# First and last expert item of a mixture-of-experts block: transposes into the result banks, earlier splits, and the last weights in other slots

## The reference

```python
def moe_ffn(h, w_router, b_router, w_gu, b_gu, w_down, b_down):   # top-4 of 32 experts
    ...
    gates = jax.nn.softmax(top_vals, axis=-1)
    ...
    def expert_block(args):
        xb, e = args
        gu = xb @ w_gu[e] + b_gu[e]                     # 1024 -> 2048
        gate, lin = gu[:, :D_EXPERT], gu[:, D_EXPERT:]
        gate = jnp.minimum(gate, 7.0)
        lin = jnp.clip(lin, -7.0, 7.0)
        act = (lin + 1.0) * (gate * jax.nn.sigmoid(1.702 * gate))
        return act @ w_down[e] + b_down[e]              # 1024 -> 1024
```

## Time and profile before

| what | value |
|---|---|
| median of 3 runs | 1746.84 us (1746.36 to 1748.47) |
| the profiled execution | 1746.15 us |
| its span in the trace | 1744.3 us |
| PE busy | 1647.6 us, 94% of the span |
| DVE, ACT, POOL busy | 62%, 48%, 8% |
| chain that ended last | PE 90%, DVE 4%, ACT 3%, DMA 2% |
| items begin, items' last scatter begins | 531.7 us, 1724.4 us |

### The profile page before, as it was taken

The page is one execution under the profiler, slowest core; times in us unless marked ns, Lnnn a source line. Parts: engine busy times, 40 slices in busy tenths (PEclk is TensorE's granted clock), DMA queues, the critical chain, the costliest instruction groups (busy, mean ns, idle before and its releaser), DMA issues.

```text
span 1744.3 us, 26775 instructions
## 1 busy us (share of the span) xinstructions
PE 1647.6 (94%) x9998; PEld 1373.1 (79%) x9998; DVE 1075.8 (62%) x1139; ACT 831.2 (48%) x844; POOL 134.8 (8%) x220
## 2 busy tenths in 40 slices
PE   6999989999966799999999999999999999999994
PEld 5876657987745688888888888888888888888882
DVE  4221553434255677777777777776777767777773
ACT  4243364434221455555546555455455554555543
POOL 0020220000000000100001000010000100001001
PEclk9999999999977899999999999999999999999997
DMA  5111123422065799999999999999999999999965
GB/s 201 49 49 49 48 97 121 145 82 79 24 261 203 240 361 365 384 364 370 369 371 373 365 375 365 368 386 369 360 371 372 375 374 365 369 370 377 364 247 162
DMA packets 134773, 477.05 MB, mean 273 GB/s; under 512 B 10242, under 2 KB 10291, under 8 KB 134707
## 3 DMA queue, kind: packets, MB, share of 16 engines
q1 hardware_dynamic: 123968, 446.72, 68.6%
q0 software_dynamic: 7168, 25.17, 6.2%
q10 hardware_dynamic: 3602, 4.69, 0.8%
HBM read 457.67 MB, written 18.87 MB: 273 GB/s over the span
## 4 chain that ended last, share of the span: by engine, by line
PE 90%; DVE 4%; ACT 3%; DMA 2%; issue 1%; ACTq 0%; SPq 0%; POOL 0%; DVEq 0%; POOLq 0%
PE psum L977 23%; PE psum L996 21%; PE psum L1019 21%; PE psum L609 17%; PE psum L788 1%; PE psum L777 1%; PE psum L971 1%; PE psum L963 1%; PE psum L765 1%; PE psum L880 1%; PE psum L900 1%; ACT ring_split L1116 1%; PE psum L914 0%; DVE ring_split L1496 0%; DMA X<-in_x 0%
## 5 line engine op out<-in xcount | busy, mean ns | idle before, releaser
L977 PEld LDWEIGHTS psum<-MIX,ring 128*128 128x128 f32 x4096 | 774.9, 190 | 100.9 <-DVE MIX L1904 0.9
L977 PE MATMUL psum<-MIX,ring 128*128 128x96 f32 x4096 | 725.6, 259 | 0.2 <-DVE MIX L1904 0.2
L1871 DVE TENSOR_TENSOR ring_split<-ring,w_hi_a 128x2048 fp32r<-128x2048 f32 x64 | 146.5, 2289 | 88.4 <-ACT w_hi_a L1363 86.6
L1877 DVE TENSOR_TENSOR ring_split<-ring,w_hi_x 128x2048 fp32r<-128x2048 f32 x64 | 146.5, 2288 | 88.3 <-ACT w_hi_x L1372 88.3
L996 PE MATMUL psum<-ring_split,xs_hi 128*96 128x512 f32 x512 | 200.3, 437 | 0.0
L1019 PE MATMUL psum<-ring_split,act_hi 128*96 128x512 f32 x512 | 199.0, 436 | 0.0
L1871 DVE TENSOR_TENSOR ring_split<-ring,w_hi_x 128x2048 fp32r<-128x2048 f32 x64 | 146.4, 2289 | 74.2 <-ACT w_hi_x L1363 74.2
L609 PE MATMUL psum<-ring_split,H_hi 128*128 128x512 f32 (+1 forms) x512 | 151.8, 380 | 0.6 <-DVE ring L1582 0.6
L1877 DVE TENSOR_TENSOR ring_split<-ring,w_hi_a 128x2048 fp32r<-128x2048 f32 x64 | 146.2, 2285 | 3.5 <-ACT w_hi_a L1372 3.5
L1372 ACT ACTIVATE w_hi_a<-ring 128x2048 fp32r<-128x2048 f32 x64 | 121.7, 1901 | 7.0 <-DMA ring<-in_w_down 7.0
L1372 ACT ACTIVATE w_hi_x<-ring 128x2048 fp32r<-128x2048 f32 x64 | 121.8, 1904 | 2.6 <-DMA ring<-in_w_down 2.6
(11 more groups left out here) (284 smaller groups left out, 2647.1 us busy)
## 6 DMA issues: line engine op xcount, KB each, us to landing
ring<-in_w_gu SPq DMA_DIRECT2D x256, 1024.0 KB, 10.2
ring<-in_w_down SPq DMA_DIRECT2D x128, 1024.0 KB, 12.1
ring<-in_w_in SPq DMA_DIRECT2D x6, 2048.0 KB, 10.5
X<-in_x SPq DMA_DIRECT2D x8, 512.0 KB, 7.9
ring<-in_w_out SPq DMA_DIRECT2D x2, 2048.0 KB, 7.7
ring<-in_w_mk SPq DMA_DIRECT2D x2, 2048.0 KB, 9.0
ring<-in_w_mv SPq DMA_DIRECT2D x2, 2048.0 KB, 7.8
ring<-in_w_mq SPq DMA_DIRECT2D x2, 2048.0 KB, 7.7
```

The costliest lines, as they stand in the source:

```text
L977: return mm(psum[:, dst, q * C:(q + 1) * C], lhsT=gate_w(k // 2)[:, k % 2, f * P:(f + 1) * P], rhs=xsT[:, k, :], start=k == 0 and q == 0, ...
L1871: v.tensor_tensor(lin_lo(c), lin_w(c), chunk_hi(c).bitcast(F32), ALU.subtract)\
L1877: v.tensor_tensor(down_lo(c), down_w(c), chunk_hi(c).bitcast(F32), ALU.subtract)\
```

## The change

On PE, `item_transpose(1)` moves to after the third lin chunk of item 0 and writes banks 6 and 7, and its wait for `s_ltt` goes. The wait for `y_out(31)` goes, and the last down writes banks 2 and 3, with its lo parts in the lin slots. SP loads the last down chunks into the lin slots, each once `lin` chunk c of item 31 is multiplied. ACT loads its table and makes `xs_hi` of item 0 before it waits for the accumulator's stores, and its first and last item are reordered; `y_out_last` reads banks 2 and 3 and writes `lin_rows`. DVE splits two lin chunks ahead of `xT_next(0)` and reads its register later; in the first item `xT_next(1)` comes early, and `xT_lo(1)` before `activate(0, 0)`. POOL gathers the first four items straight from `src_row`, without index copies, the first ahead of its register read.

```diff
@@ SP @@
-                sp.wait_ge(s_dused, 4 * m + c + 1)
-                load_down(d, c)
+                sp.wait_ge(s_lused, 4 * m + c + 1)
+                sp.dma_start(lin_w(c), down_rows(d, c)).then_inc(s_m[8 + c], 16)
@@ PE @@
-            def item_transpose(t):
+            def item_transpose(t, to=T0):
...
                     x_last.then_inc(s_lused, 1)
+                    if c == 2 and isinstance(t, int) and t == 0:
+                        item_transpose(1, Y0)
...
-            def down_chunk(v, c, gate):
+            def down_chunk(v, c, gate, lo=down_lo, to=Y0):
...
             lin_transpose(0)
-            pe.wait_ge(s_ltt, 1)
-            item_transpose(1)
             lin_and_gate(1)
...
             down_and_gate(m, transpose_next=False)
-            pe.wait_ge(s_yrow, m)
             for c in range(4):
-                down_chunk(m + 1, c, False)
+                down_chunk(m + 1, c, False, lin_lo, L0)
@@ ACT @@
             def lin_hi(t, c):
                 act.wait_ge(s_m[8 + c], 16 * t + 16)
-                if not isinstance(t, int) or t > 0:
+                if isinstance(t, int):
+                    if t > 0:
+                        act.wait_ge(s_lused, c + 1)
+                else:
                     act.wait_ge(s_dused, 4 * t + c - 3)
...
             def down_hi(v, c, last=False):
-                act.wait_ge(s_m[c], 16 * v)
                 if last:
+                    act.wait_ge(s_m[8 + c], 16 * v + 16)
                     act.wait_ge(s_dused, 4 * v + c - 3)
+                    go(chunk_hi(c), lin_w(c), ACT.Copy).then_inc(s_dhi, 1)
...
+            def y_out_last(v):
+                go(gate_last, slot_gate[:, bass.ds(v - 1, 1)], ACT.Copy).then_inc(s_gcur, 1)
+                act.wait_ge(s_gcur, v)
+                act.wait_ge(s_dused, 4 * v + 4)
+                go(lin_rows.rearrange("p (a b) -> p a b", a=2), psum[0:C, 2:4, :], ACT.Copy,
+                   scale=gate_last).then_inc(s_yrow, 1)
...
+            nc.scalar.preload_act_table_set("sigmoid_and_others")
+            xT_hi(0)
             act.wait_ge(s_accinit, 16 * TT)
+            lin_hi(0, 2)
+            lin_hi(0, 3)
             act.wait_ge(s_items, 1)
             m = act.value_load(last_item_i[0:1, 0:1], min_val=E - 1, max_val=MAX_ITEMS - 1)
-            nc.scalar.preload_act_table_set("sigmoid_and_others")
-            xT_hi(0)
-            lin_hi(0, 2)
-            lin_hi(0, 3)
+            lin_hi(1, 0)
+            lin_hi(1, 1)
             lin_out(0)
+            xT_hi(1)
             sigmoid(0, 0)
-            xT_hi(1)
-            lin_hi(1, 0)
+            lin_hi(1, 2)
             a_hi(0, 0)
-            lin_hi(1, 1)
-            lin_hi(1, 2)
+            lin_hi(1, 3)
             sigmoid(0, 1)
-            lin_hi(1, 3)
...
             down_hi(m + 1, 2, last=True)
+            sigmoid(m, 1)
+            down_hi(m + 1, 3, last=True)
+            a_hi(m, 1)
             y_out(m)
-            sigmoid(m, 1)
-            a_hi(m, 1)
-            down_hi(m + 1, 3, last=True)
-            y_out(m + 1)
+            y_out_last(m + 1)
@@ DVE @@
-            m = dve.value_load(last_item_i[0:1, 0:1], min_val=E - 1, max_val=MAX_ITEMS - 1)
             lin_lo_part(0, 0)
+            lin_lo_part(0, 1)
             xT_next(0)
             xT_lo(0)
             xT_place(0)
-            for c in range(1, 4):
-                lin_lo_part(0, c)
+            m = dve.value_load(last_item_i[0:1, 0:1], min_val=E - 1, max_val=MAX_ITEMS - 1)
+            lin_lo_part(0, 2)
+            lin_lo_part(0, 3)
+            xT_next(1, 6)
+            lin_lo_part(1, 0)
+            lin_lo_part(1, 1)
             st = Steps(0)
             bias(st, 0)
             gate_in(st, 0, 0)
             lin_in(st, 0)
+            xT_lo(1)
             activate(st, 0, 0)
-            xT_next(1)
-            lin_lo_part(1, 0)
-            xT_lo(1)
+            xT_place(1)
             a_lo(0, 0)
-            xT_place(1)
-            lin_lo_part(1, 1)
             lin_lo_part(1, 2)
...
-            down_lo_part(m + 1, 0)
+            last_down_lo_part(m + 1, 0)
             a_lo(m, 0)
-            down_lo_part(m + 1, 1)
-            down_lo_part(m + 1, 2)
+            last_down_lo_part(m + 1, 1)
+            last_down_lo_part(m + 1, 2)
             gate_in(st, m, 1)
             activate(st, m, 1)
             a_lo(m, 1)
-            down_lo_part(m + 1, 3)
+            last_down_lo_part(m + 1, 3)
@@ POOL @@
+            def first_gather(t):
+                if t > 0:
+                    pool.wait_ge(s_xt, t)
+                g.indirect_dma_start(out=x_rows, out_offset=None, in_=rows_dram[:, :],
+                                     in_offset=bass.IndirectOffsetOnAxis(src_row[:, t:t + 1], 0))\
+                    .then_inc(s_xrow, 16)
...
+            pool.wait_ge(s_rowsout, 16 * TT)
+            pool.wait_ge(s_items, 1)
+            first_gather(0)
+            n = pool.value_load(n_items_i[0:1, 0:1], min_val=E, max_val=MAX_ITEMS)
...
-            scatter(late + 3)
+            scatter(late + 3, lin_rows)
             pool.wait_ge(s_scat, 16 * n)
```

More of the change, by code:

```diff
@@ L288, in build @@
         gate_cur = KDb[0:C, 288:289]
+        gate_last = KDb[0:C, 290:291]
         bias_cur = KDb[:, 296:312]
@@ L1017, in down_chunk @@
                     rows_ = (act_lo if a else act_hi)[:, f, :]
-                    cols_ = (down_lo(c) if b else chunk_hi(c))[:, k2, half * 512:half * 512 + 512]
-                    x_last = mm(psum[0:C, Y0 + half, :], lhsT=rows_, rhs=cols_, start=f == 0 and n == 0,
+                    cols_ = (lo(c) if b else chunk_hi(c))[:, k2, half * 512:half * 512 + 512]
+                    x_last = mm(psum[0:C, to + half, :], lhsT=rows_, rhs=cols_, start=f == 0 and n == 0,
                                 stop=f == KT - 1 and n == 2, skip_group_check=True)
@@ L1365, in down_hi @@
             def down_hi(v, c, last=False):
-                act.wait_ge(s_m[c], 16 * v)
                 if last:
+                    act.wait_ge(s_m[8 + c], 16 * v + 16)
                     act.wait_ge(s_dused, 4 * v + c - 3)
+                    go(chunk_hi(c), lin_w(c), ACT.Copy).then_inc(s_dhi, 1)
                 else:
+                    act.wait_ge(s_m[c], 16 * v)
                     act.wait_ge(s_lused, 4 * v + c + 1)
-                go(chunk_hi(c), down_w(c), ACT.Copy).then_inc(s_dhi, 1)
+                    go(chunk_hi(c), down_w(c), ACT.Copy).then_inc(s_dhi, 1)
             def lin_out(t):
@@ L1872, in lin_lo_part, with last_down_lo_part @@
                     .then_inc(s_llo, 1)
+            def last_down_lo_part(w, c):
+                dve.wait_ge(s_dhi, 4 * w + c + 1)
+                v.tensor_tensor(lin_lo(c), lin_w(c), chunk_hi(c).bitcast(F32), ALU.subtract)\
+                    .then_inc(s_dlo, 1)
             def down_lo_part(w, c):
@@ L1878, in down_lo_part, with t_bank, xT_next @@
                     .then_inc(s_dlo, 1)
-            def t_bank(u):
-                return psum[:, 4 + u, 0:4 * C].rearrange("p (k c) -> p k c", k=4)
+            def t_bank(u, at=4):
+                return psum[:, at + u, 0:4 * C].rearrange("p (k c) -> p k c", k=4)
             def over_c(a):
                 return a.unsqueeze(2).broadcast_to([P, 4, C])
-            def xT_next(t):
+            def xT_next(t, at=4):
                 dve.wait_ge(s_xt, t + 1)
@@ L2078, in _ @@
             pool.sem_inc(s_const, 1)
-            pool.wait_ge(s_items, 1)
-            n = pool.value_load(n_items_i[0:1, 0:1], min_val=E, max_val=MAX_ITEMS)
-            def gather(t):
-                if isinstance(t, int) and t == 0:
-                    ch.link(g.tensor_copy(gather_idx, src_row[:, 0:1]))
-                else:
-                    pool.wait_ge(s_xt, t)
-                    g.tensor_copy(gather_idx, src_row[:, bass.ds(t, 1)]).then_inc(s_gidx, 1)
+            def first_gather(t):
[4 more added lines that the diff above has]
+                    .then_inc(s_xrow, 16)
+            def gather(t):
+                pool.wait_ge(s_xt, t)
+                g.tensor_copy(gather_idx, src_row[:, bass.ds(t, 1)]).then_inc(s_gidx, 1)
                 pool.wait_ge(s_rowsout, 16 * TT)
-                if not (isinstance(t, int) and t == 0):
-                    pool.wait_ge(s_gidx, t)
+                pool.wait_ge(s_gidx, t)
                 g.indirect_dma_start(out=x_rows, out_offset=None, in_=rows_dram[:, :],
@@ L2106, in scatter @@
                                      out_offset=bass.IndirectOffsetOnAxis(scatter_idx, 0),
-                                     in_=y_rows, in_offset=None, compute_op=ALU.add).then_inc(s_scat, 16)
+                                     in_=rows_, in_offset=None, compute_op=ALU.add).then_inc(s_scat, 16)
             pool.sem_inc(s_yfree, 1)
-            for t in range(4):
-                gather(t)
+            pool.sem_inc(s_gidx, 3)
+            for t in range(1, 4):
+                first_gather(t)
             scatter(1)
```

6 lines of the change are left out of this document (3 added, 3 removed).

## The result

The changed kernel takes 1734.57 us (median of 6 runs, 1732.56 to 1735.28), the kernel before, run beside it, 1746.92. The ratio is 0.9927, with a 95% interval from 0.9914 to 0.9940: 12.8 us faster, clear of noise. 1732.8 had been forecast, with a range of 1730.0 to 1736.5. The profiled execution of the changed kernel took 1732.56 us, the fastest of its runs; its span is 1730.7 us where it was 1744.3.

What follows compares the result with a forecast made beforehand. PE was taken to bound the loop, so only its stalls outside it could go. Gains of 7.15 us at the head and 6.9 at the tail, 14.05 off 1746.15, plus 0.7 to the median, gave 1732.8, range 1730.0 to 1736.5.

Steps and rivals of the forecast that it cites:

- PE sets the time, and only its stalls at the ends can go: Item loop: PE busy all 36.20 us of a period, so only its idle time outside the loop can go.
- Before the first lin matmul: Head, item 0: stores and table load leave the chain, DVE late next; PE starts at 545.1, gain 1.5 us, bounds 0 to 1.8.
- the sum: Whole kernel: 7.15 us at the head plus 6.9 us at the tail, 14.05 us.
- Between lin of item 0 and lin of item 1: Head: only xT_lo(1) remains behind lin_in; first gate matmul at 577.1 instead of 584.25, gain 7.15 us, the 1.5 included.
- The gate weights: Item 1, head: chunk 0, issued 0.8 us earlier, lands at 575.7, 1.4 us ahead of need.
- The slow clock behind the stall: Head, before item 1: slow start at 1.2 GHz kept; rival that it goes, 1.5 to 2 us more gain, chance 0.12.
- Before the last down: Tail: last down starts at 1704.3 without a gap at full clock; gain 6.9 us, 4.33 waiting and 12 x 0.2 slow clock.
- The chain for act_lo: Tail, last item: starts at 1704.3, a_lo ends near 1708.6, 1.3 us before PE needs it.
- POOL's margin: Tail, last scatter: POOL could start it at 1716.7, PE's side at 1717.5, so PE decides by 0.8 us.
- The rival: Tail: POOL sets the tail if the first of two scatters is held or takes over 5.6 us; 1734.5, chance 0.17.
- The level: Whole kernel: profiled execution 1746.15 - 14.05 = 1732.1; the median stands 0.7 above it, so 1732.8.

Runs made afterwards that it cites:

- head and tail alone: Two kernels: the changed kernel with every last-item edit undone, 1741.45 us (0.9965 to before); the kernel before with those edits alone, 1740.44 us (0.9957).
- the second profile: The changed kernel, unaltered, run once more beside the run before it on the same chip: 1734.87 us, 0.9929 to before.
- the one with only one split ahead: Changed kernel with xs_lo and xsT before lin_in, half of item 0's second gate half inside lin, and VectorE's second split after item 0's rows: 1734.80 us.
- the kernel where PE had no pause there at all: Kernel with gates inside lin and one split first, with SyncE's eight loads for item 1 in the order their slots come free: 1725.26 us, 0.9873 to before.

## Why the prediction was right, point by point

- **PE sets the time, and only its stalls at the ends can go**: right; head and tail alone give 6.1 and 7.5 us and add up, and the loop takes as long as before to the hundredth.
- **Before the first lin matmul**: 545.1 was forecast, 545.05 came; DVE was late next, as said. The gain of 1.5 us was real as a start, and mis-sized as a gain: the sum counted it whole. The clock came up at 550.33 and not sooner than before (549.96), so PE spent 1.9 us more at half speed, and 0.6 us of the start were left, just what the transposes then cost (0.7 in the sum). This is the one term of the sum that failed: `lin_in` was forecast at 572.85 and came at 573.65, 0.8 us later.
- **Between lin of item 0 and lin of item 1**: 4.25 us from `lin_in` to the first gate matmul were forecast (572.85 to 577.1), 4.20 came (573.65 to 577.85). The gate weights were in time, as forecast, and by little: chunk 0 was issued at 567.63, not 0.8 sooner, and the kernel with xs_lo and xsT before `lin_in` ran into it.
- **The slow clock behind the stall** was taken as kept, and it was. Its fall came at 577.6 here and at 577.3 before; what it costs differs by run more than I allowed.
- **Before the last down**: no gap, 0.231 us a matmul (0.236 in the sum, which counted up to ScalarE's row); 6.9 us were forecast, 13.36 - 6.40 = 6.96 came. The chain for act_lo, forecast to end at 1708.6, ended at 1701.61 + 0.56 = 1702.17, 6.4 us sooner, which is the head's shift.
- **POOL's margin** was real: the index copy took 0.18 us, not 2.20, and ended at 1709.84, 0.4 us before the rows it waited with (1709.12 + 1.11). The rival was not reached. The reason for the shrunken margin is below.
- **The level**: profile against profile, 13.59 us less were measured, 14.05 forecast. Median against median the gain is 12.35. The sum was lifted by the 0.7 us between the profiled execution of before and its median; the changed kernel's profile lies 2.0 us under its median, and has an early begin of the items and the short slow stretch, which the second profile of it, 1.6 us longer, has not. That the forecast of 1732.8 lies 1.8 us under the median is for the most part this.

## What to carry to other kernels

Where two waits stand one behind the other, removing either alone can show nothing: take both, and check by putting each back. A gain that falls into a stretch of slow clock is worth what the clock's rise leaves of it, and slow clock inside a wait costs nothing, so don't count it twice; and where a buffer is freed sooner, look at the queue of the loads too, because the load behind four others in program order goes no sooner than they do. Unrolled first and last passes deserve their own schedule: 22 us of 1747 lay there, none in the loop.

## What the runs showed of the hardware

**An indirect DMA's issue on GpSimd is held while VectorE runs a split, an operation with two SBUF inputs.** The gather of item 1 on GpSimd, in the changed kernel and in the one with only one split ahead:

```profile
540.68 2.31 POOL L2104 DMA_INDIRECT H<-rows_scratch,KDb  x1 [6.96 <-PE psum L964]
```

```profile
542.46 0.91 POOL L2108 DMA_INDIRECT H<-rows_scratch,KDb  x1 [6.96 <-PE psum L964]
```

It took 2.31 us where VectorE's split ran until 542.20, and 0.91 where no split ran and VectorE took rows from PSUM (542.20 to 543.22). VectorE's last split of the changed kernel, and its scatter for item 29, which stands as those of the loop do:

```profile
1702.08 2.28 DVE L1890 TENSOR_TENSOR ring_split<-ring,w_hi_x 128x2048 fp32r<-128x2048 f32 x1
```

```profile
1671.92 1.59 POOL L2131 DMA_INDIRECT acc_scratch<-H,KDb  x1 [27.43 <-ACT H L1407]
```

The scatter at 1703.60 took 2.07 us, with VectorE's last split until 1704.36; the one at 1711.02, with VectorE idle, took 1.42. Those of the loop take 1.6, as the one for item 29, for whose first 0.26 us a split ran (until 1672.18). So the gather, the scatter at 1703.60 and that for item 29 overlapped a split by 1.52, 0.76 and 0.26 us, and took 1.40, 0.65 and 0.17 us longer than with none. The shorter VectorE operations on SBUF inputs that follow in the loop (128x384, from 1672.10 on) add nothing that can be seen, so not every operation of that kind holds an issue under way. The gather and the scatter at 1703.60 ended 0.8 and 1.3 us after the split did. The prediction had left this open for the issue of a transfer; the Trainium skill's page "SBUF — State Buffer" (on the two sides of the memory) has VectorE and GpSimd block one another for a whole instruction, and for the splits these runs agree. Here it took 0.5 us of POOL's margin, and nothing from the time.

**The clock after a rest is not the same from run to run.** Of one kernel, one profile had PE at 1.2 GHz for 3.4 us and another for 6.8 us at the same place; from one set of lin's transposes to the next it took 28.15 us in the first (572.79 to 600.94) and 29.62 in the second (573.09 to 602.71), 1.5 us more. Starting lin 1.5 us sooner moved the rise by nothing, and 1.6 us more moved it by 3 us. Before item 1 the slow stretch was gone only in the kernel where PE had no pause there at all.
